# Latent norms in the projection's tail, rope rows packed four heads to a tile, and a reordered index front, in a two-block hybrid transformer kernel

## The reference

```
def mla_mixer(h, cos, sin, w_in, q_norm, kv_norm, w_q_b, w_kv_b, w_out):
    proj = h @ w_in
    c_q = proj[..., :256]
    c_kv = proj[..., 256:384]
    k_rope = apply_rope(proj[..., 384:], cos, sin)
    q = (rms_norm_2(c_q, q_norm) @ w_q_b).reshape(b, s, 16, 96)
    q_rope = apply_rope(q[..., 64:], cos[:, :, None, :], sin[:, :, None, :])
    qk = concatenate([q[..., :64], q_rope], axis=-1)
    kv = (rms_norm_2(c_kv, kv_norm) @ w_kv_b).reshape(b, s, 16, 128)
    k = concatenate([kv[..., :64], broadcast(k_rope)], axis=-1)
    v = kv[..., 64:]
    y = blocked_attention(qk, k, v, 96 ** -0.5, CHUNK)
    return y.reshape(b, s, 1024) @ w_out
```

## Time and profile before

| | us |
|---|---|
| Median of 3 runs | 2978.51 (2975.18 to 2979.47) |
| The profiled execution: its own time | 2976.7 |
| The profiled execution: its span | 2974.9 |
| PE busy | 2766.3, 93% |
| DVE busy | 1358.0, 46% |
| ACT busy | 838.7, 28% |
| POOL busy | 582.6, 20% |

### The profile page before, as it was taken

How to read it: one execution, slowest core, us unless ns; L and a number is a source line. 1 busy time by engine, 2 the same in 40 slices (tenths; PEclk the granted TensorE clock), 3 DMA queues, 4 the chain that set the end, 5 groups by cost and what they waited for, 6 DMA issues and landing times. The chain is left out here.

```text
span 2974.9 us, 39094 instructions
## 1 busy us (share of the span) xinstructions
PE 2766.3 (93%) x16402; PEld 2188.2 (74%) x16402; DVE 1358.0 (46%) x1875; ACT 838.7 (28%) x1239; POOL 582.6 (20%) x387
## 2 busy tenths in 40 slices
PE   6989997769999799999989999999999879899998
PEld 4768855658888588887857888878888635688887
DVE  3454568353332643435454434454333466543433
ACT  2232135231122321223253212232222336422222
POOL 1000123032111221212301302122112120120302
PEclk7999989979999999999999999999999989999999
DMA  7241210113222223223202333233232310233221
GB/s 250 73 156 42 78 39 1 57 57 99 93 92 85 82 88 99 87 87 100 85 15 85 99 99 99 75 109 98 87 98 85 97 24 1 63 108 94 94 89 50
DMA packets 248959, 247.14 MB, mean 83 GB/s; under 512 B 18628, under 2 KB 244744, under 8 KB 248528
## 3 DMA queue, kind: packets, MB, share of 16 engines
q1 hardware_dynamic: 248578, 244.58, 26.2%
q10 hardware_dynamic: 206, 0.06, 0.0%
HBM read 241.46 MB, written 2.12 MB: 82 GB/s over the span
## 5 line engine op out<-in xcount | busy, mean ns | idle before, releaser
L383 DVE TENSOR_TENSOR ffn_wt_lo<-ring,ffn_wt_hi 128x2048 fp32r<-128x2048 f32 (+1 forms) x166 | 413.8, 2493 | 258.0 <-ACT ffn_wt_hi L368 258.0
L368 ACT CAST ffn_wt_hi<-ring 128x2048 fp32r<-128x2048 f32 (+1 forms) x166 | 307.6, 1853 | 772.4 <-PE bank L561 772.4
L1060 POOL TENSOR_TENSOR ffn_act_hi<-ffn_act,const 128x512 fp32r<-128x512 f32 x110 | 216.9, 1972 | 1325.0 <-DVE ffn_act L1051 1325.0
L561 PE MATMUL bank<-feat_hi,ffn_wt_hi 128*128 128x512 f32 x1056 | 331.8, 396 | 20.0 <-DVE feat_lo L442 11.5
L561 PE MATMUL bank<-feat_lo,ffn_wt_hi 128*128 128x512 f32 x1056 | 328.9, 393 | 0.0
L561 PE MATMUL bank<-feat_hi,ffn_wt_lo 128*128 128x512 f32 x1056 | 328.7, 393 | 0.0
L561 PE MATMUL bank<-ffn_act_hi,ffn_wt_hi 128*128 128x512 f32 x880 | 271.5, 390 | 0.9 <-POOL ffn_act_lo L1062 0.9
L561 PE MATMUL bank<-ffn_act_lo,ffn_wt_hi 128*128 128x512 f32 x880 | 271.0, 389 | 0.0
L561 PE MATMUL bank<-ffn_act_hi,ffn_wt_lo 128*128 128x512 f32 x880 | 270.9, 389 | 0.0
L561 PEld LDWEIGHTS bank<-feat_hi,ffn_wt_hi 128*128 128x128 f32 x1056 | 198.5, 189 | 68.4 <-issue 11.3
L561 PEld LDWEIGHTS bank<-feat_lo,ffn_wt_hi 128*128 128x128 f32 x1056 | 199.7, 189 | 44.0
(11 more groups left out here) (602 smaller groups left out, 4357.7 us busy)
## 6 DMA issues: line engine op xcount, KB each, us to landing
ring<-in_ffn_w_gate SPq DMA_DIRECT2D x44, 1024.0 KB, 5.3
ring<-in_ffn_w_up SPq DMA_DIRECT2D x44, 1024.0 KB, 5.4
ring<-in_ffn_w_down SPq DMA_DIRECT2D x32, 1024.0 KB, 5.1
ring<-in_ada_w SPq DMA_DIRECT2D x24, 1024.0 KB, 6.3
ring<-in_ffn_w_down SPq DMA_DIRECT2D x16, 768.0 KB, 4.4
ring<-in_w_ffn_gate SPq DMA_DIRECT2D x11, 1024.0 KB, 5.3
ring<-in_w_ffn_up SPq DMA_DIRECT2D x11, 1024.0 KB, 5.3
ring<-in_w_in SPq DMA_DIRECT2D x8, 1024.0 KB, 5.4
```

Of the source, the lines that this page charges most:

```text
L368: self.nc.scalar.copy(self.wh[:, n % 2, 0:words], K.ring[:, n % RING, 0:words]).then_inc(K.high_done, 1)
L383: self.nc.vector.tensor_tensor(self.wl[:, n % 2, 0:words], K.ring[:, n % RING, 0:words], self.wh[:, n % 2, 0:words].bitcast(F32), ALU.subt ...
L561: lasts[m] = pe.matmul(outs[m], a, b, start=n == 0 and p == 0, stop=end and p == 2)
L1060: nc.gpsimd.tensor_tensor(ah[:, f, :], a[:, i % 2, :], K.k("ones")[:, 0:1].broadcast_to([P, T]), ALU.mult)
```

## The change

- The norm stage of the latents is gone. Squares, sums, roots, reciprocals, spreads and the products with gain stand at the end of the input stage, behind its last projection. The key-value latent is projected before the rope rows, whose weights shrink from 128 to 64 columns.
- The weights of queries, keys and values come through the ring, as six chunks. Those of the queries are split: 64 plain rows a head (`mla_qw`), two heads to a tile of 128 rows, and 32 rope rows a head (`mla_rw`), four heads to a tile.
- The swapped halves of the rope rows come from a matmul with a constant permutation ("halves") in place of DMAs. DVE rotates tiles of 128 x 512; POOL does nothing here. 16 DMAs of 64 KB move the rotated rows to partitions 64 to 95 of `mQ`, and one DMA of 1 MB copies the key's rope rows to all heads.
- DVE works out the angles and rotates the key inside the preparation stage (`angles`, `key`).
- In the front stage TensorE takes the bonus sums and variances first, then four dots of block 3, two gates, three spreads, four dots, two gates, and the last spread. ACT's order follows. The spreads use banks 5, 6, 7, 5.

```
-        spread_banks = [K.bank[b] for b in (5, 6, 0, 1)]
+        spread_banks = [K.bank[b] for b in (5, 6, 7, 5)]
...
-                step(n_gate)
-                step(n_gate + 1)
                 bonus_sum(2)
                 bonus_sum(3)
                 variances()
+                dots(range(8, 12))
+                step(n_gate)
+                step(n_gate + 1)
+                for p in range(3):
+                    spread(p)
+                dots(range(12, 16))
                 step(n_gate + 2)
                 step(n_gate + 3)
-                dots(range(8, 16))
-                spreads()
+                spread(3)
...
+    def tensor(pe):
+        S = box["split"]
+        pe.wait_ge(box["wl"], 1)
+        product3(pe, K.bank[5][0:64, :], (((box["hi"][:, k, :], box["lo"][:, k, :]), S.feature(pe, k, False)) for k in range(KD))
                  ).then_inc(box["pe"], 1)
+        pe.wait_ge(box["sq"], 3)
+        for at, tiles_in in ((0, (0, 1)), (4, (2,))):
+            for b in range(TB):
+                last = product(pe, K.bank[6][:, at + b:at + b + 1], [(sq[n][:, b * P:(b + 1) * P], K.k("ones")[:, 0:1]) for n in tiles_in])
+        last.then_inc(box["sums"], 1)
+        pe.wait_ge(box["inv"], 1)
+        for at, bank in ((0, 4), (4, 7)):
+            for b in range(TB):
+                last = pe.matmul(K.bank[bank][:, b * P:(b + 1) * P], box["col"][:, at + b:at + b + 1].broadcast_to([P, P]), K.k("ident"),
+                                 start=True, stop=True)
+            last.then_inc(box["spread"], 1)
...
     def scalar(act):
+        for n in range(3):
+            act.wait_ge(box["read"], n + 1)
+            act.activation(sq[n], latents[n], ACT.Square).then_inc(box["sq"], 1)
+        act.wait_ge(box["sums"], 1)
+        for at, width in ((0, 256), (4, 128)):
+            act.activation(box["col"][:, at:at + 4], K.bank[6][:, at:at + 4], ACT.Sqrt, bias=K.k("eps")[:, 0:1], scale=1.0 / width).then_inc(box["root"], 1)
...
     def vector(dve):
+        dve.wait_ge(box["pe"], 1)
+        for half in (slice(0, ROPE), slice(ROPE, 2 * ROPE)):
+            nc.vector.tensor_tensor(B.kr[half, :], K.bank[5][half, :], K.rs[half, :], ALU.mult)
+        dve.wait_ge(box["root"], 2)
+        nc.vector.reciprocal(box["col"][:, :], box["col"][:, :]).then_inc(box["inv"], 1)
...
+        steps = ([("q", t) for t in range(8)] + [("r", 0), ("r", 1), ("s", 0), ("r", 2), ("s", 1), ("r", 3), ("s", 2), ("k", 0), ("s", 3)]
+                 + [("k", t) for t in range(1, 8)] + [("v", t) for t in range(8)])
...
             @block.sync
             def _(sp):
+                sp.wait_ge(s_kr, 1)
+                sp.dma_start(B.K[64:96, :, :], B.kr[0:ROPE, :].unsqueeze(1).broadcast_to([ROPE, MH, T])).then_inc(s_moved, 16)
+                K.stream(sp, plan.end("mla_v"))
                 for g in range(4):
+                    sp.wait_ge(s_rot, g + 1)
+                    for j in range(4):
+                        sp.dma_start(B.Q[64:96, 4 * g + j, :], K.h[32 * j:32 * j + 32, g, :]).then_inc(s_moved, 16)
+                K.stream(sp, plan.end("mla_v") + RING)
+                sp.wait_ge(s_moved, 16 * 17)
...
+                    elif kind == "s":
+                        v.tensor_tensor(turned(t), bank[:, :], B.sin[:, :], ALU.mult).then_inc(s_v, 1)
+                        v.tensor_tensor(rope(t), rope(t), B.cos[:, :], ALU.mult)
+                        dve.drain()
+                        v.tensor_tensor(rope(t), rope(t), turned(t), ALU.add).then_inc(s_rot, 1)
...
+    w_q, w_kv = io["mla_w_q_b_2"][0].rearrange("(k p) (h c) -> k p h c", p=P, c=QK), io["mla_w_kv_b_2"][0].rearrange("p (h two d) -> two p h d", two=2, d=64)
+    plan.add("mla_qw", 2, lambda c: w_q[c][:, :, 0:64], marks=1, split=False)
+    plan.add("mla_rw", 2, lambda c: w_q[c][:, :, 64:QK], marks=1, split=False)
+    plan.add("mla_k", 1, lambda c: w_kv[0], marks=1, split=False)
+    plan.add("mla_v", 1, lambda c: w_kv[1], marks=1, split=False)
```

More of the change, by code:

```diff
@@ L1639, in variances, with spread @@
                     last.then_inc(s_var, 1)
[L1641 to L1650, removed]
+                def spread(p):
+                    if p == 0:
+                        pe.wait_ge(s_inv, 1)
+                        pe.wait_ge(s_bonus, 4)
+                    if p == 3:
+                        pe.wait_ge(s_done, 1)
+                    for b in range(TB):
+                        for h, hh in enumerate((slice(0, HD), slice(HD, P))):
+                            last = pe.matmul(spread_banks[p][hh, b * P:(b + 1) * P],
+                                             root[:, p, 2 * b + h:2 * b + h + 1].broadcast_to([P, HD]), idt, start=True, stop=True)
+                    last.then_inc(s_spread, 1)
                 for n in range(n_iq):
@@ L2488, in mla_in_stage @@
     R = slice(64, 96)
+    sq = [K.h[:, n, :] for n in range(1, 4)]
+    latents = (B.cq[:, 0, :], B.cq[:, 1, :], B.ckv[:, :])
+    pe, act = nc.tensor, nc.scalar
     def sems(st):
[L2491 to L2494, removed]
+        (box["w"], box["wh"], box["wl"], box["pe"], box["pos"], box["ang"], box["sq"], box["sums"], box["root"], box["inv"],
+         box["spread"]) = st.sems("wr", "wr_high", "wr_low", "rope", "pos", "angle", "latent_squares", "latent_sums", "latent_roots",
+                                  "latent_inverses", "latent_spread")
+        box["wr"] = st.sb("wr", [P, KD, 64])
+        box["hi"], box["lo"] = st.sb("wr_hi", [P, KD, 64], F32R), st.sb("wr_lo", [P, KD, 64], F32R)
@@ L2540, in scalar @@
[L2540 to L2542 removed]
+        act.activation(B.sin[:, :], box["ang_t"][:, :], ACT.Sin)
+        act.activation(B.cos[:, :], box["ang_t"][:, :], ACT.Sin, scale=0.5)
     def vector(dve):
[L2545 to L2547 removed]
@@ L2607, in _ @@
             @block.tensor
             def _(pe):
-                pe.wait_ge(K.mla_weights_in, 48)
-                for t, (rows, _, pairs, _, _) in enumerate(steps):
-                    if t >= 8:
-                        pe.wait_ge(s_s if t % 2 else s_v, (t - 8) // 2 + 1)
-                    product(pe, K.bank[t % 8][0:rows, :], pairs).then_inc(s_pe, 1)
-            wide = lambda ap: ap[R, :].unsqueeze(1).broadcast_to([ROPE, 4, T])
-            turned = lambda g: (B.Q[R, 4 * g:4 * g + 4, :], swap[R, 4 * (g % 2):4 * (g % 2) + 4, :])
@@ L2640, in _ @@
             @block.scalar
             def _(act):
-                nc.scalar.copy(B.K[R, :, :], B.kr[R, :].unsqueeze(1).broadcast_to([ROPE, MH, T]))
-                evacuate(act, 1)
+                for n, (kind, t) in enumerate(steps):
+                    bank = K.bank[n % 8]
+                    if by_scalar[n]:
+                        act.wait_ge(s_pe, n + 1)
+                    if kind == "q":
+                        nc.scalar.mul(plain(B.Q, t)[0], bank[0:64, :], scale).then_inc(s_s, 1)
+                    elif kind == "k":
+                        nc.scalar.copy(plain(B.K, t)[0], bank[0:64, :]).then_inc(s_s, 1)
+                    elif kind == "r":
+                        nc.scalar.mul(rope(t), bank[:, :], scale).then_inc(s_s, 1)
+                    elif kind == "v" and t % 2:
+                        nc.scalar.copy(B.V[:, t // 2, 512:1024], bank[:, :]).then_inc(s_s, 1)
```

185 lines of the change are left out of this document (89 added, 96 removed).

## The result

The changed kernel took 2939.34 us (median of 4 runs, 2936.68 to 2941.08); beside it, on the same chip, the kernel before took 2976.85 (4 runs, 2969.28 to 2979.47). The ratio is 0.9883, 95% interval [0.9868, 0.9899], so 35 us are saved, between 30 and 39 (the two medians by themselves would give 0.9874). The profiled executions took 2938.13 and 2976.7 us, spans 2936.3 and 2974.9. The forecast was 2945, range 2938 to 2956.

What follows compares the result with a forecast made beforehand. Order of work and DVE's queue were taken to bound the stretch before the second block's attention, with TensorE behind. Terms -14.3 - 18.0 + 1.8 - 1.5 - 1.5 = -33.5 us gave 2945 against the 2978.5 median, range 2938 to 2956.

Steps and rivals of the forecast that it cites:

- ramp: Attention's start: shorter idle gap mostly removes its 5.1 us stretch at low clock; -1.5 us, bounds 0 and -2.5.
- Term 1: Input stage's tail, query tiles' end to preparation's first matmul: 32.9 us becomes 18.6, -14.3.
- Term 2: Preparation: 44 matmuls by 0.866 us plus evacuation and barrier, 57.1 us becomes 39.1, -18.0.
- the dip: Preparation's first matmuls: one stretch at the lower clock after the tail's idle time, +1.8 us, bounds 0 and 3.6.
- Term 3: TensorE's clock: +1.8 us at the preparation's first matmuls, -1.5 us at the attention's start.
- Term 4: Front stage: 6.60 us DVE wait goes, last dots come later; -1.5 us, bounds +0.9 and -6.6.
- The branch with full clock: Front stage: TensorE at full clock from the spreads on, the same sum ending at 439.2, -3.8 us.
- Late key weights: Preparation: key weights queue behind the 1 MB broadcast, 0 to +5 us; 0.18 together with late banks or last move.
- Serial moves: Preparation: 16 small DMAs run one after another at 3.3 us and end the stage, +36, 2981 us; chance 0.02.
- Half clock through the preparation: TensorE stays at 1.2 GHz all through the preparation, +36.3, 2981 us; chance 0.03 for a large part.
- DVE as the bound: Preparation: rotations at twice 2.1 us give DVE 35 us, still under 38; +0 to +2 us, no separate chance.

Runs made afterwards that it cites:

- experiment 7: Changed kernel with each of the four half-swap permutation products done twice, eight more TensorE records in the preparation; 2942.55 us, ratio 0.9898.
- latent part alone: Changed kernel with the front stage's old order, so only the latent part of the change; 2943.24 us, ratio 0.9906 to the kernel before.
- experiment 8: Changed kernel with the first DVE operation of each of the four rotations done three times; 2943.26 us, ratio 0.9893, preparation +2.00 us.
- front alone: Kernel before with only the front stage's new order; 2969.03 us (11 runs) against 2973.29, ratio 0.9988.
- moves in turn, experiment 9: Changed kernel with SP waiting for each of the 16 moves of rope rows before issuing the next; 2961.16 us, ratio 0.9949.
- experiment 11: Changed kernel with nine unread products in TensorE's idle time of the tail, three behind the sums, six behind the spreads; 2938.33 us, ratio 0.9884.
- rotation thrice: Changed kernel with DVE's first operation of each of the four rotations done three times; 2943.26 us, ratio 0.9893.
- experiment 12: Changed kernel with POOL's last four adds of head scores in the front on 8 columns in place of 512; 2939.65 us, ratio 0.9886.
- experiment 10: Changed kernel with SP issuing the key and value weights only after the key's broadcast has landed; 2937.96 us, ratio 0.9875.

## Why the prediction was right or wrong

The local gains add to -13.53 - 14.28 - 2.4 - 4.35 = -34.6, less up to 1.5 given back in the first attention, against -33.5 forecast and 35 [30, 39] measured. The mechanism held; the sizes of the terms were off in both directions. That the sum came out so near is in part luck: tail and preparation gave 2.7 us less than their terms, ramp and front 3.8 us more.

- **Term 1, -14.3, measured -13.5.** Right, and its parts are shown: norms 4.7, rope order 3.6, key and angles 4.2, each by an experiment, and the load wait of 1.8 by its row alone, with some 0.7 of overlap. The 24 sums took 2.73 us (2.7) and the handovers 0.74 (0.95). Off were the spreads: I took eight records in 1.5 us, as only the query half is waited for; but all 16 records took 3.78 at 1.2 GHz, since the third gain product waits for the second half, and the wait from their end to the preparation is 1.27: 5.05 us for the 3.96 of the sum (1.5 + 2.16 + 0.3).
- **Term 2, -18.0, with the dip -16.2, measured -14.3.** The 88 records at the upper clock are as forecast; experiment 7 shows that they are the bound. What the sum has no term for: at three places the code drains TensorE (lets it finish) ahead of the signal that frees weight chunks, and there the rows show it idle for 0.37, 0.26 and 0.29 us. The records beside such a gap also lose the 0.2 us by which they otherwise overlap (a record takes some 0.6 us and they start 0.43 apart), which makes some 1.5 us by estimate. The kernel without a dip (latent part alone) took 40.54 us, 1.4 more than the 39.1 of the sum. No run leaves the drains out, so that this is read from rows and not shown by an experiment; nor does any run part the 14.3 us between the packed tiles, the order and POOL's absence. DVE was costed well (26.7 for 25.0 us), its slack far too high (experiment 8).
- **Term 3, dip +1.8, measured 2.2 (16.21 - 13.97), and ramp -1.5, measured -2.4** (the offset of the attention's second score products). Both in their bounds. For the ramp one doubt stays: front alone had none in spite of its old wait of 3.01 us. With a wait near 3 us or more the ramp was there in three profiles of four (both of before, and moves in turn, where TensorE stood 18.37 us); with 0.95 to 1.63 us in none of ten. So behind the shorter wait it never came at the attention's first products, where otherwise it came most times. But the low clock can come a little later: in fill (experiment 11) and in rotation thrice it fell from the eighth microsecond of the attention on and cost 1.4 and 4 us. What the forecast missed is where the preparation's dip begins: in the spreads (0.50), behind 24 records of one column and a wait of 0.74 us, and not at the preparation's first matmul. In the latent part alone the spreads ran at 0.55 too, and the preparation behind them at 1.00: what varied is whether the low clock lasted.

The page "TensorE: Matmul & The Clock Gate" of the Trainium skill (section "HAM oscillation — how this bites in real kernels") says that idle gaps between bursts make each burst start cold. Here that is a tendency and no more: front alone started its attention at 1.00, right behind the same gap at which before started at 0.50.

- **Term 4, -1.5 (middle of +0.9 and -3.8), measured -4.35.** The step that failed is the choice of the middle. The branch with full clock "from the spreads on" was right in substance: the clock was 0.52 to 427 and 1.00 from there, the last y tile ended at 438.70 (forecast of that branch 439.2), the mask at 436.5 (436.4). Why the clock rose there is not shown. The trace of before showed 1.2 GHz there, and I weighed that as if it could last. That the adds of POOL slow DVE I had not foreseen, but it decided nothing: it only hid the wait that I had expected ahead of the last y tiles, and experiment 12 brought that out.
- **Rivals.** Late key weights (0.18 with its companions): did not come, and experiment 10 shows that its loads could start 3.5 us later. Serial moves: they overlapped; run one by one they cost +17.4 and not +36, as one takes 1.96 us and not 3.3. The Trainium skill's page "SBUF — State Buffer" (section "The DMA setup-cost knee") gives some 2 us to each small transfer; the lone move, 1.9 us to landing, agrees with it. Moves issued without a wait between them still landed in 2.0 us each but started 0.6 us apart, so that the fixed part overlapped. Half clock through the preparation: 0.95 was granted. DVE as the bound: not here, but nearer than the rival said.
- **The comparison itself.** The prediction was set against a profiled execution that carried about 5.5 us of dips in places that the change does not touch (1395, 1503 to 1555, 2553), which the changed kernel's profile lacked. The one at 2553 stood in two of the new kernels too (moves in turn and rotation thrice), so it comes and goes. That the two spans differ by 38.6 and not by 33 to 35 is mostly this. Why the dips at 1395 and 1503 to 1555 stood in both profiles of before and in none of the twelve other kernels, front alone among them, stays open: its many runs speak for chance, the profiles against it, and nothing here decides.

## What to carry to other kernels

A barrier with one engine's chain ahead of it costs what no other engine can do meanwhile: ask of each operation in a tail whether the next stage could cover it (here 4.2 us of angles and key), and put the product whose weights come last behind one whose weights are there (3.6 us). When operations beside another engine's get slower, look for the wait that follows when they are fast again before you count them as lost. And before terms of 1 to 3 us are read from two spans, lay the two traces side by side row for row and look for shifts where the code is the same.

## What the runs showed of the hardware

- DVE beside POOL's adds of 128x512: an operation with both operands in SBUF took 1.60 us for 0.69, one with a further operand (L1796) 0.95 to 1.10 for 0.75; one with an operand in PSUM kept 0.74. All four slow ones ended 0.55 us after the POOL add beside them. With POOL's adds narrowed all were back. The Trainium skill says the same ("SBUF — State Buffer", section "SBUF: two separate sides"): DVE with two SBUF inputs and GpSimd share a pair of ports and exclude each other. The rotations of the kernel before show it as well: DVE's add of 6.43 us ended 2.1 us after POOL's multiply did, and such an add took 2.28 us by itself.

```profile
2422.85 6.54 POOL L2654 TENSOR_TENSOR mQ<-mQ,mcos 32x2048 f32<-32x2048 f32 x1
...
2425.10 6.43 DVE L2625 TENSOR_TENSOR mQ<-mQ,h 32x2048 f32<-32x2048 f32 x1
```

- The same wait of TensorE, 2.93 and 3.01 us behind the same work, was followed by 5.1 us at a granted clock of 0.50 in two executions and at 1.00 in a third.
- Moves of 64 KB between partitions: waited for one by one, 1.9 us to landing and one every 1.96 us; issued without a wait, one every 0.6 us (the issue itself took 0.59), each landing in 2.0.
- Four loads of 1 MB issued in a row on SP stood 5.16 us ahead of a barrier, when the moves before them had all landed (experiment 9): their issues took 0.4, 0.6, 1.2 and 2.9 us, longer with each.
